# Scores of the first attention layer: from whole 32-bit products to three passes over high and low parts

## The reference, cut to what matters

```python
    qx = apply_rope(qx, cos, sin)
    kx = apply_rope(kx, cos, sin)
    near = jnp.abs(kj - BLOCK - qi) <= WINDOW          # keys of the previous, own and next block of 128
    def attend_block(args):
        q, k, v, m = args
        s_loc = jnp.einsum("bqhgd,bkhd->bhgqk", q, k).astype(F32) * scale
        s_loc = jnp.where(m, s_loc, -jnp.inf)
        s_ctx = jnp.einsum("bqhgd,bchd->bhgqc", q, kc).astype(F32) * scale
        p = softmax_with_sink(jnp.concatenate([s_loc, s_ctx], axis=-1), sink_b).astype(v.dtype)
        return (jnp.einsum("bhgqk,bkhd->bqhgd", p[..., :3 * BLOCK], v)
                + jnp.einsum("bhgqc,bchd->bqhgd", p[..., 3 * BLOCK:], vc))
```

## Time and profile before

| | |
|---|---|
| Median of 3 runs | 2527.21 us (2522.06 to 2530.29) |
| The profiled execution: its time | 2527.9 us |
| Its span | 2526.6 us |
| PE busy | 2357.1 us (93%) |
| PEld busy | 1983.8 us (79%) |
| DVE busy | 1845.5 us (73%) |
| ACT busy | 1069.9 us (42%) |
| POOL busy | 625.5 us (25%) |

### The profile page before, as it was taken

How to read it: one execution, slowest core, us unless ns; L and a number is a source line. 1 busy time by engine, 2 the same in 40 slices (tenths; PEclk the granted TensorE clock), 3 DMA queues, 4 the chain that set the end, 5 groups by cost and what they waited for, 6 DMA issues and landing times.

```text
span 2526.6 us, 33463 instructions
## 1 busy us (share of the span) xinstructions
PE 2357.1 (93%) x12399; PEld 1983.8 (79%) x12399; DVE 1845.5 (73%) x3422; ACT 1069.9 (42%) x1910; POOL 625.5 (25%) x408
## 2 busy tenths in 40 slices
PE   7989999999999989999999998999688989899997
PEld 5768999999899989999999986787455767455555
DVE  7899898999999977888888875524666454155554
ACT  3332333333488843333333344321566333344452
POOL 4110367778722232322333302000000100000001
PEclk9999999999999999999999999999899999999999
DMA  6537557788788999999999951121000112000001
GB/s 250 187 133 250 167 185 233 244 249 254 254 311 317 331 360 368 363 338 362 359 370 372 353 191 50 51 67 59 1 1 1 51 46 101 32 19 20 10 1 67
DMA packets 162227, 465.94 MB, mean 184 GB/s; under 512 B 15505, under 2 KB 72977, under 8 KB 159633
## 3 DMA queue, kind: packets, MB, share of 16 engines
q1 hardware_dynamic: 100368, 304.40, 34.3%
q0 software_dynamic: 36864, 134.23, 14.9%
q10 hardware_dynamic: 24832, 25.17, 3.1%
HBM read 411.31 MB, written 52.43 MB: 184 GB/s over the span
## 4 chain that ended last, share of the span: by engine, by line
PE 70%; DVE 14%; DMA 5%; ACT 4%; issue 4%; POOL 2%; DVEq 0%; ACTq 0%
PE psum L427 6%; PE psum L429 5%; PE psum L428 5%; PE psum L571 5%; PE psum L573 5%; PE psum L572 5%; PE psum L435 4%; PE psum L437 4%; PE psum L436 4%; DMA arena<-hidden 4%; PE psum L544 3%; PE psum L863 2%; PE psum L453 2%; POOL weights_low L1955 2%; PE psum L883 2%
## 5 line engine op out<-in xcount | busy, mean ns | idle before, releaser
L940 ACT ACTIVATE weights_high<-arena 128x1024 fp32r<-128x1024 f32 x355 | 374.8, 1056 | 430.1 <-PE psum L573 293.7
L1394 DVE TENSOR_TENSOR weights_low<-arena,weights_high 128x1024 fp32r<-128x1024 f32 x266 | 334.0, 1256 | 217.2 <-ACT weights_high L940 216.3
L435 PE MATMUL psum<-x_high,weights_high 128*128 128x384 f32 x1024 | 351.8, 344 | 27.0 <-POOL weights_low L1955 18.6
L571 PE MATMUL psum<-hidden_high,weights_high 128*128 128x384 f32 x1024 | 344.8, 337 | 11.2 <-DVE hidden_low L1656 8.0
L437 PE MATMUL psum<-x_high,weights_low 128*128 128x384 f32 x1024 | 344.5, 336 | 0.0
L436 PE MATMUL psum<-x_low,weights_high 128*128 128x384 f32 x1024 | 344.2, 336 | 0.0
L573 PE MATMUL psum<-hidden_high,weights_low 128*128 128x384 f32 x1024 | 343.3, 335 | 0.0
L572 PE MATMUL psum<-hidden_low,weights_high 128*128 128x384 f32 x1024 | 343.1, 335 | 0.0
L427 PE MATMUL psum<-x_high,weights_high 128*128 128x512 f32 (+1 forms) x696 | 278.1, 400 | 24.0 <-DVE weights_low L1394 19.0
L1955 POOL TENSOR_TENSOR weights_low<-arena,weights_high 128x1024 fp32r<-128x1024 f32 x89 | 229.0, 2573 | 200.3 <-ACT weights_high L940 199.8
L429 PE MATMUL psum<-x_high,weights_low 128*128 128x512 f32 (+1 forms) x696 | 273.0, 392 | 0.0
(11 more groups left out here) (237 smaller groups left out, 4199.3 us busy)
## 6 DMA issues: line engine op xcount, KB each, us to landing
arena<-in_stream SPq DMA_DIRECT2D x227, 512.0 KB, 4.1
arena<-in_v_rows SPq DMA_DIRECT2D x128, 512.0 KB, 7.1
arena<-in_ada_w SPq DMA_DIRECT2D x48, 512.0 KB, 3.3
hidden<-arena SPq DMA_DIRECT2D x128, 192.0 KB, 4.7
router<-arena SPq DMA_DIRECT2D x12, 2048.0 KB, 10.0
arena<-hidden SPq DMA_DIRECT2D x128, 192.0 KB, 7.8
arena<-router ACTq DMA_DIRECT2D x16, 1536.0 KB, 22.6
arena<-in_pair_w SPq DMA_DIRECT2D x8, 576.0 KB, 3.8
```

Source lines behind the costliest of these rows:

```text
L435: PE.matmul(bank[b][:, 0:N], wh[u % 2][:, k, :], xh[:, k, PICKED:T], start=k == 0, stop=False)
L571: PE.matmul(out, wh[w][:, n, :], hh[:, r, :], start=e == 0, stop=False)
L940: ACT.activation(wh[u % 2], slots[u % RING], AF.Copy).then_inc(*tick("weights_high", u))
L1394: DVE.tensor_tensor(wl[u % 2], slots[u % RING], wh[u % 2].bitcast(F32), ALU.subtract).then_inc(*tick("weights", u))
```

## The change: scores in three passes

PE now computes each piece of the scores in three passes over rounded operands instead of one whole 32-bit product. Four places make the operands. ACT rounds the keys once (`kh_a`) and the queries of a chunk into one of two buffers (`qh_a`, in `q_high`); DVE subtracts (`kl_a` over the keys' own place, `ql[i]` over the queries' own place, in `q_low`). The keys and chunk 0 are split ahead of the stage, the queries of chunk `i + 1` in the pair of tile 2 of chunk `i`. The new buffers lie in places of the weight ring and its split copies, so the first unit of `a_out` is split at the end of the stage and its third is loaded once the last scores are done.

```diff
+    ql = [halves(f"queries{i}_low", first, TC) for i, first in enumerate(qr_at)]
+    qh_a = [halves(f"queries_high{i}", first, TC) for i, first in enumerate((64 * T + T // 2, 63 * T))]
+    kh_a, kl_a = halves("keys_high", 4 * T, 2, TC), halves("keys_low", 40 * T, 2, TC)
...
-            for sc, rows in both:
-                last = PE.matmul(sc[:, T:TC], qr[i][rows, t * P:(t + 1) * P], kt[rows, p, T:TC], start=True, stop=True)
+            def scores(out, keys, masked):
+                for n, (qs, ks) in enumerate(((qh_a[i % 2], kh_a), (qh_a[i % 2], kl_a), (ql[i], kh_a))):
+                    for sc, rows in both:
+                        last = PE.matmul(sc[:, out], qs[rows, t * P:(t + 1) * P], ks[rows, p, keys], start=n == 0,
+                                         stop=n == 2 and not masked)
+                return last
+
+            last = scores(slice(T, TC), slice(T, TC), False)
             if t < NT:
                 first = tiles[0]
-                for sc, rows in both:
-                    PE.matmul(sc[:, lo:T], qr[i][rows, t * P:(t + 1) * P], kt[rows, p, first * P:(tiles[-3] + 1) * P],
-                              start=True, stop=False)
+                scores(slice(lo, T), slice(first * P, (tiles[-3] + 1) * P), True)
...
+        def q_high(i):
+            if i >= 2:
+                ACT.wait_ge(*at("scored", ("a", 12 * (i - 2) + 10)))
+            else:
+                ACT.wait_ge(*at("unit", unit("a_q", 6 + i)))
+            ACT.wait_ge(*at("roped", ("q", i)))
+            ACT.wait_ge(*at("qr_ctx", i))
+            ACT.activation(qh_a[i % 2], qr[i], AF.Copy).then_inc(*tick("q_high", i))
+
+        ACT.wait_ge(*at("weights", unit("a_q", 7)))
+        for p in range(2):
+            ACT.wait_ge(*at("roped", ("k", p)))
+            ACT.wait_ge(*at("kt_ctx", p))
+            ACT.activation(kh_a[:, p, :], kt[:, p, :], AF.Copy).then_inc(*tick("k_high", p))
+        q_high(0)
...
+            else:
+                ACT.wait_ge(*at("scored", ("a", j)))
+                high_weights(unit("a_out"))
             a_turn(j)
             a_turn(j + 1)
+            if j % 12 == 4 and j < 84:
+                q_high(j // 12 + 1)
...
+        def q_low(i):
+            DVE.wait_ge(*at("q_high", i))
+            DVE.tensor_tensor(ql[i], qr[i], qh_a[i % 2].bitcast(F32), ALU.subtract).then_inc(*tick("q_low", i))
+
+        for p in range(2):
+            DVE.wait_ge(*at("k_high", p))
+            DVE.tensor_tensor(kl_a[:, p, :], kt[:, p, :], kh_a[:, p, :].bitcast(F32), ALU.subtract).then_inc(
+                *tick("k_low", p))
+        q_low(0)
         a_rope(("q", 7), qr[7], 6)
...
                 a_maxima(j + 3)
             if i and t == 4:
                 a_gates(i - 1, 0)
+            if t == 2 and i < 7:
+                q_low(i + 1)
+            if j == A_JOBS - 2:
+                low_weights(unit("a_out"))
```

More of the change, by code:

```diff
@@ L236, in write, with halves @@
     tmp = area(90, T)
-    qr = [columns_at(8 * T + c * TC, TC) for c in range(5)] + [columns_at(72 * T + c * TC, TC) for c in range(2)] + [
-        columns_at(88 * T, TC)]
+    qr_at = [8 * T + c * TC for c in range(5)] + [72 * T + c * TC for c in range(2)] + [88 * T]
+    qr = [columns_at(first, TC) for first in qr_at]
+    def halves(name, first, *shape):
+        return nc.alloc_sbuf_tensor_at(name, [P, *shape], F32R, offset=SBUF_AT + first * 4)[
+            tuple(slice(None) for _ in range(len(shape) + 1))]
+    ql = [halves(f"queries{i}_low", first, TC) for i, first in enumerate(qr_at)]
+    qh_a = [halves(f"queries_high{i}", first, TC) for i, first in enumerate((64 * T + T // 2, 63 * T))]
+    kh_a, kl_a = halves("keys_high", 4 * T, 2, TC), halves("keys_low", 40 * T, 2, TC)
     prob = [columns_at(first * T, 641) for first in (36, 38, 46, 90)]
@@ L693, in a_scores @@
                     PE.wait_ge(*at("roped", ("q", n)))
-            for sc, rows in both:
-                last = PE.matmul(sc[:, T:TC], qr[i][rows, t * P:(t + 1) * P], kt[rows, p, T:TC], start=True, stop=True)
+                for n in range(2):
+                    PE.wait_ge(*at("k_low", n))
+            if t == 0:
+                PE.wait_ge(*at("q_low", i))
+            def scores(out, keys, masked):
[5 more added lines that the diff above has]
+            last = scores(slice(T, TC), slice(T, TC), False)
             if t < NT:
                 first = tiles[0]
-                for sc, rows in both:
-                    PE.matmul(sc[:, lo:T], qr[i][rows, t * P:(t + 1) * P], kt[rows, p, first * P:(tiles[-3] + 1) * P],
-                              start=True, stop=False)
+                scores(slice(lo, T), slice(first * P, (tiles[-3] + 1) * P), True)
                 sides = [0] * (t > 0) + [2] * (t < NT - 1)
@@ L1204, in scalar @@
             u = unit("a_q", i)
-            high_weights(u + 1)
+            if i < 7:
+                high_weights(u + 1)
             if i == 0:
@@ L1739, in vector @@
             u = unit("a_q", i)
-            low_weights(u + 1)
+            if i < 7:
+                low_weights(u + 1)
             if i:
@@ L1982, in load_unit @@
         def load_unit(u):
+            if u == unit("a_out", 2):
+                SP.wait_ge(*at("scored", ("a", A_JOBS - 2)))
             if RING <= u < N_UNITS:
```

## The result

| | before | changed |
|---|---|---|
| Median of 4 runs each | 2528.75 us | 2558.89 us (2553.92 to 2563.05) |
| Ratio to before | | 1.0128 (1.0108 to 1.0149) |
| The profiled execution: time, span | 2527.9, 2526.6 us | 2553.92, 2552.6 us |
| Stage: from PE's first scores to its first value products of the last chunk (1773.20 to 1963.06 before, 1772.09 to 1988.42 changed) | 189.86 us | 216.33 us |
| DVE, ACT busy in it | 125.0, 117.0 us | 131.0, 125.0 us |

What follows compares the result with a forecast made beforehand. Engine order in the attention stage, not a full engine, was taken as the bound; passes -5.8, splits +23.8, clock +4, start +2.8 and end +1.0 gave +25.8 us, so 2553 us, range 2538 to 2568.

Steps and rivals of the forecast that it cites:

- What bounds: Attention stage: no engine is full, order decides; the chain runs mostly through PE, with ACT's exponents and DVE's maxima.
- The passes: PE's scores: three rounded passes save 0.07 us on 256 columns, 0.12 on 384; -5.8 us over 8 chunks.
- The splits in each chunk: DVE's subtraction waits for ACT's rounding and delays tile 4's maxima; tile 5's scores 3.4 us late, +23.8 in seven chunks.
- the walk: Step-by-step timing of one chunk, from ACT's rounding at 1887.54 to tile 5's scores, 3.4 us late.
- The clock: PE in the stalls: four or five falls to half clock, some 1.2 us each, +4 us net; ends 0 and 12.
- the third rival: PE's clock falls in every chunk and stays down: +12 to +16 in place of +4, 2563 to 2566 us; 13%.
- Ahead and behind: Before the stage, DVE's three subtractions delay first scores, +2.8 us; at its end DVE's weight split delays the gate, +1.0.
- The sum: Whole kernel: -5.8 + 23.8 + 4 + 2.8 + 1.0 = +25.8 us, giving 2553 us, 1.0% slower.
- Halves one after the other: PE's rounded passes: the two halves do not run beside one another, +25 in place of -5.8, 2584 us; 6%.
- loads that show: PE's weight loads wait for the stream ahead, so the passes gain 0 in place of -5.8, 2559 us; 7%.
- Absorbed stall: ACT rounds in a gap ahead of the exponents, DVE waits for nothing: -2.6, 2524.6 us; 6% no change, 3% faster.
- A stall of 1 us: Passes not much shorter, stall only 1 us a chunk since DVE's normalisation was not urgent: +7, 2534 us; 6%.

Runs made afterwards that it cites:

- passes only: The changed kernel without the query splits of chunks 1 to 7, all chunks using chunk 0's operands: 2530.22 us, 1.0003 of the kernel before.

## Why the prediction was right, point by point

- **What bounds.** Right. The loop through PE, DVE and ACT set the stage, and not the busy shares.
- **The passes.** Right. A chunk at full clock is 0.80 us shorter without the stall, as worked out from rounded passes of 0.12 us for 256 columns. That makes 6.3 us in all, against 5.8 taken. The 8.3 us by which the full-clock steps shortened hold 2.0 more, which the loop made up behind the stalls (2.29 for 2.49 us in the step to tile 5).
- **The splits in each chunk.** Right, with 3.43 us for 3.4 in the walk, and 24.0 for 23.8 in sum. Only "behind that the loop goes on in the old rhythm" was not so: with 0.28 us made up in the next two steps, a stall costs 3.15 us net, 22.1 in seven. The walk's own steps came out too: DVE waited 3.48 us, and the maxima of tile 4 were released by nothing but DVE's own queue. Moving the subtraction alone gave back 2.70 of the 3.43.
- **The clock.** The mechanism was right, and the size was off: +4 was taken and +10.3 measured. I had counted four or five falls of a single stretch in seven stalls. It fell behind every one, in five of the seven for some 10.2 us, as in 1875.8 to 1886.0. So the number of falls was that of the third rival and of my upper end, each chunk, and the price of 10.3 lies just under the 12 of both. (That rival's time was added up wrongly: +12 to +16 in place of +4 gives 2561 to 2565, not 2563 to 2566; the median lies below either.) I had also not seen that shorter passes make the thin stretch of tiles 0 and 1 thinner, and bring falls there without any stall: in the run with passes only there were six behind the first chunk, where before had two.
- **Ahead and behind.** +2.9 for +2.8, and +0.9 for +1.0. The first scores came at 1772.09 and not at 1776, since the part ahead of the copy was shorter. At the end it went as said: ACT's weight split fitted into its gap, and DVE's held the gate up.
- **The sum.** +25.8 was taken and +29.4 measured. The stall came out 0.2 larger, the shorter steps 2.5 larger as a gain, the clock 6.3 larger, and the first exponents came 0.4 earlier. The term that was off is the clock, and part of its error was cancelled by luck by the shorter steps. It was luck, too, that the profiled execution came out at 2553.9, next to the 2553.7 forecast: the part ahead of the stage was 4 us shorter in it; the median is 2558.9.
- **The rivals.** Halves one after the other, and loads that show: no, by the pairs of records 0.12 us apart. Absorbed stall: no in this order; with the rounding two pairs and the subtraction one pair earlier, yes, and the time is that of before. A stall of 1 us: no, 3.43.

## What to carry to other kernels

Where engines run in a tight loop, ask of each instruction that is added what stands behind it in its queue and when its input is there; the same 0.9 us of work on each of two engines cost 3.4 us in one place and nothing that could be measured one and two pairs earlier. A faster product on an engine that waits within the loop may give its gain back through the clock; look at the granted clock in the windows of that stage before and after, and not at the busy share. Products that nobody reads, put in the waits of TensorE, can be worth their place. Here filling one of two thin places gave nothing, since the clock then fell in the other, and filling both gave back 7.5 us.

## What the hardware showed that I had not expected

- Half clock came in the change in stretches of some 10.2 us behind five of the seven stalls (as 1875.8 to 1886.0), and of 13.6 and 6.8 us behind the other two. In the kernels without a stall the thin stretch of tiles 0 and 1 brought, behind the first two chunks, single stretches of 3.4 us.
- Six extra products a chunk, 1.4 us of work at full clock, took 5.2 us out of the stage and 16 more ahead of it another 5.8. With both, the stage ran at 0.99 of the full clock, against 0.94 in the kernel before.
- A rounded pass on 64 partitions, two halves beside one another, takes the 0.12 us of one on 128 partitions for 256 columns: the three passes take 0.36 us where the whole product took 0.43.
